# Shared last groups, a query projection one group ahead, V slots 0, 2, 5 or 0 on VectorE, 2 KB weight rows, and V sums ahead of two output projections

## The reference

```python
q = (xt @ w_q).reshape(t, PEER_HEADS, 2, PEER_HALF)
s = jnp.einsum("thpd,hpnd->thpn", q, sub_keys)          # 8 heads, 2 x 128 keys
s1, i1 = lax.top_k(s[:, :, 0], 16); s2, i2 = lax.top_k(s[:, :, 1], 16)
cand = s1[..., :, None] + s2[..., None, :]              # 256 candidates, again the best 16
idx, g = ..., softmax(top_s)                            # 16 experts a head and token
u = jnp.take(u_tab, ic, axis=0)                         # 16384 x 1024 table
a = jnp.einsum("cd,chkd->chk", xc, u)
w = gc * jax.nn.gelu(a, approximate=False)
vv = jnp.take(v_tab, ic, axis=0)
out = jnp.einsum("chk,chkd->cd", w, vv)
```

## Time and profile before

| | |
|---|---|
| median of 3 runs | 1631.06 us (1630.27 to 1631.42) |
| the profiled execution | 1630.2 us, of which its span is 1628.2 us |
| busy in the span | PE 1330.9 us, DVE 1073.0, POOL 1013.0, ACT 468.4 |
| moved by DMA | 619.20 MB, mean 380 GB/s; gathers 536.94 MB, SP's transfers 81.36 MB |
| granted TensorE clock, mean | 0.907 of full speed |

### The profile page before, as it was taken

How to read it: one execution, slowest core, us unless ns; L and a number is a source line. 1 busy time by engine, 2 the same in 40 slices (tenths; PEclk the granted TensorE clock), 3 DMA queues, 4 the chain that set the end, 5 groups by cost and what they waited for, 6 DMA issues and landing times.

```text
span 1628.2 us, 17186 instructions
## 1 busy us (share of the span) xinstructions
PE 1330.9 (82%) x4558; PEld 768.0 (47%) x4558; DVE 1073.0 (66%) x2529; ACT 468.4 (29%) x1427; POOL 1013.0 (62%) x1099
## 2 busy tenths in 40 slices
PE   7999789888885899887877789989868877777775
PEld 7887544444552564354444366545434432222222
DVE  4248689988775445638778835674878985555555
ACT  0203343333332222433233222451333321111112
POOL 0006677777547656667666654675776777777764
PEclk9999898999998999899888899999999988888887
DMA  9519999999999999999999999999999999999997
GB/s 336 185 53 372 397 399 409 405 404 405 379 391 378 396 393 394 409 405 390 401 401 403 401 376 384 397 397 393 400 403 409 409 411 409 410 409 410 410 409 272
DMA packets 224232, 619.20 MB, mean 380 GB/s; under 512 B 18914, under 2 KB 90652, under 8 KB 224156
## 3 DMA queue, kind: packets, MB, share of 16 engines
q0 software_dynamic: 147456, 536.94, 83.7%
q1 hardware_dynamic: 76699, 81.36, 15.0%
HBM read 617.17 MB, written 1.05 MB: 380 GB/s over the span
## 4 chain that ended last, share of the span: by engine, by line
PE 36%; DMA 22%; POOL 13%; issue 12%; DVE 9%; ACT 5%; POOLq 0%; SPq 0%; DVEq 0%; ACTq 0%
DMA u_ring<-in_peer_u_dram,idx_now 20%; PE acc L795 18%; PE tile L765 13%; POOL u_ring L520 7%; POOL v_ring L520 7%; DVE u_ring L1010 4%; ACT diag L610 2%; DMA v_ring<-in_peer_v_dram,idx_now 2%; ACT gelus L604 2%; PE xf L765 1%; PE tile L897 1%; PE tile L924 1%; PE tile L892 1%; PE tile L928 0%; PE tile L787 0%
## 5 line engine op out<-in xcount | busy, mean ns | idle before, releaser
L795 PE MATMUL acc<-v_ring,diag 128*128 128x512 f32 x1780 | 852.9, 637 | 118.5 <-ACT diag L610 74.0
L1010 DVE CUSTOM_DVE_ANT_0 u_ring<-u_ring,xf 128x1024 f32<-128x1024 f32 x512 | 613.2, 1216 | 270.2 <-DMA u_ring<-in_peer_u_dram,idx_now 267.2
L520 POOL DMA_INDIRECT v_ring<-in_peer_v_dram,idx_now x512 | 495.4, 968 | 294.5 <-issue 121.9
L795 PEld LDWEIGHTS acc<-v_ring,diag 128*128 128x128 f32 x1780 | 359.9, 207 | 581.3 <-issue 565.9
L520 POOL DMA_INDIRECT u_ring<-in_peer_u_dram,idx_now x512 | 503.3, 983 | 173.4 <-issue 126.5
L596 ACT ACTIVATE gelus<-dots 128x8 f32<-128x8 f32 x64 | 13.4, 209 | 515.4 <-DVE dots L1010 515.4
L610 ACT ACTIVATE diag<-ident,gelus 128x128 f32<-128x128 f32 x448 | 137.8, 388 | 2.1
L765 PE MATMUL tile<-w_ring,fT 128*128 128x256 f32 x480 | 110.4, 384 | 6.4 <-DVE fT L1159 6.4
L765 PEld LDWEIGHTS tile<-w_ring,fT 128*128 128x128 f32 x480 | 92.0, 192 | 30.3 <-issue 12.0
L604 ACT ACTIVATE gelus<-gelus,gates 128x1 f32<-128x1 f32 x512 | 102.1, 281 | 4.9 <-ACT gelus L596 3.3
L714 ACT ACTIVATE gexp<-best,gstat 128x16 f32<-128x16 f32 x32 | 9.8, 307 | 306.9 <-DVE best L1300 306.9
(11 more groups left out here) (170 smaller groups left out, 1043.0 us busy)
## 6 DMA issues: line engine op xcount, KB each, us to landing
w_ring<-in_peer_wq_dram SPq DMA_DIRECT2D x23, 1024.0 KB, 16.5
w_ring<-in_w_out_dram SPq DMA_DIRECT2D x12, 1024.0 KB, 16.8
w_ring<-in_w_kv_dram SPq DMA_DIRECT2D x12, 1024.0 KB, 16.9
u_ring<-in_peer_u_dram,idx_now POOLq DMA_INDIRECT x512, 11.5
v_ring<-in_peer_v_dram,idx_now POOLq DMA_INDIRECT x512, 11.0
w_ring<-in_w_in_b_dram SPq DMA_DIRECT2D x8, 1024.0 KB, 16.5
u_ring<-in_w_in_a_dram SPq DMA_DIRECT2D x4, 1024.0 KB, 12.2
w_ring<-in_w_mem_kv_dram SPq DMA_DIRECT2D x4, 1024.0 KB, 15.4
```

The lines of the kernel that those rows point to most:

```text
L520: pool.indirect_dma_start(ring[:, s, :], None, rows_[:, :], bass.IndirectOffsetOnAxis(idx_now[:, column + s:column + s + 1], 0), element_o ...
L795: ins = pe.matmul(acc[:, 512 * n:512 * n + 512], diag[:, par * G + s, :], v_ring[:, s, 512 * n:512 * n + 512], start=(first and s == 0), s ...
L1010: dve.tensor_tensor_reduce(u_ring[:, s, :], u_ring[:, s, :], xf[:, :], 1.0, 0.0, ALU.mult, ALU.add, dots[:, par * G + s:par * G + s + 1])\
```

## The change

1. **Who adds V slots.** `FOLDED` becomes [0]. In the groups `BUSY` (0 to 3 of phase 0, 0 to 9 of phases 1 and 2) DVE adds slots 0, 2 and 5 and PE the other five. In the last two groups DVE adds 1, 3, 5, 7 and 1, 3, 5, 6, 7 behind all dots (`fold_late` in place of `add_last`), with `read_sum` ahead of slot 6 of group 63. The final rows are made and stored in two halves of the columns.
2. **Query ahead.** The query projection and ACT's copy of it become a step of their own ("query"), which stands at the end of the side list of the group before its route. Some routes of phase 0 move by a group.
3. **Gathers.** `idx_now`, its copies and the loops on POOL go; gathers read `idx_all`. Phase 1 waits for the heads that a group needs.
4. **2 KB rows.** Pieces of out, q, k, v and qf are 512 rows by 512 columns: 1 MB again, in rows of 2 KB. A tile of 256 columns needs two pieces, which serve two tiles; both are held until the second tile is done.
5. **V sums ahead.** For groups 0 and 1 of phase 0, PE does the side steps up to the first "out", then the V sums, then the rest.

```diff
-FOLDED = [7]
+FOLDED = [0]
+LOOPED = GROUPS * PHASES - 2
+BUSY = [*range(0, 4), *range(GROUPS, GROUPS + 10), *range(2 * GROUPS, 2 * GROUPS + 10)]
+BUSY_FOLDED = [0, 2, 5]
+LATE_FOLDED = {LOOPED: [1, 3, 5, 7], LOOPED + 1: [1, 3, 5, 6, 7]}
...
+    pe_start, start = queried(pe_start), queried(start)
+    side[0, 0][0:0] = [("query", 0, 1)]
+    for key in list(side):
+        for step in [s for s in side[key] if s[0] == "route" and s != ("route", 0, 1)]:
...
+                side[key].remove(step)
+                side[key][0:0] = [step]
+                side[group_before(*key)].append(("query", *step[1:]))
...
+def split_side(ph, g):
+
+    steps = SIDE[ph, g]
+    cut = len(steps)
+    if (ph, g) in ((0, 0), (0, 1)):
+        cut = next(n for n, step in enumerate(steps) if step[0] == "out")
+    return steps[:cut], steps[cut:]
...
+        if len(key) == 4:
+            return blocks[:, key[3] * (KD // 2):(key[3] + 1) * (KD // 2), col:col + 2 * PC]
...
-            return HEADS * (ph // 2) + (HEADS if ph == 1 else h + 1)
+            return HEADS * (ph // 2) + h + 1
...
+            def gather_v(q, s):
+                if q == 0:
+                    filled(pool, LAST_USE[HELD[(G + s) // 2]])
+                elif s in folded(q - 1):
+                    pool.wait_ge(v_folded, folds_before(q - 1) + folded(q - 1).index(s) + 1)
+                else:
+                    pool.wait_ge(v_added, sums_before(q - 1) + summed(q - 1).index(s) + 1)
+                gather(v_rows, v_ring, q, s, v_landed)
...
+                elif kind == "query":
+                    _, ph, h = step
+                    filled(act, ("q", ph, h))
+                    act.activation(q_rows[:, :], bank(("q", ph, h))[:, 0:PC], ACT.Copy).then_inc(q_copied, 1)
...
-                    for step in SIDE[ph, g]:
+                    ahead, behind = split_side(ph, g)
+                    for step in ahead:
                         side(step)
                     if g == 0 and ph:
                         pe.wait_ge(acc_read, ph)
                     group(GROUPS * ph + g, g % 2, first=(g == 0))
+                    for step in behind:
+                        side(step)
```

More of the change, by code:

```diff
@@ L57, with folded, summed, counted @@
 NW = 5
-NI = 4
 WARM_UP = 15
-FOLDED = [7]
+FOLDED = [0]
 SUMMED = [s for s in range(G) if s not in FOLDED]
 GP, GD = len(SUMMED), len(FOLDED)
-PE_LAST = G // 2
+LOOPED = GROUPS * PHASES - 2
+BUSY = [*range(0, 4), *range(GROUPS, GROUPS + 10), *range(2 * GROUPS, 2 * GROUPS + 10)]
+BUSY_FOLDED = [0, 2, 5]
+LATE_FOLDED = {LOOPED: [1, 3, 5, 7], LOOPED + 1: [1, 3, 5, 6, 7]}
+def folded(q):
+    if not isinstance(q, int):
+        return FOLDED
+    return BUSY_FOLDED if q in BUSY else LATE_FOLDED.get(q, FOLDED)
+def summed(q):
+    return [s for s in range(G) if s not in folded(q)]
+def counted(q, slots):
+    if isinstance(q, int):
+        return sum(len(slots(n)) for n in range(q))
+    each, base = len(slots(LOOPED - 1)), GROUPS * (PHASES - 1) + 1
+    more = counted(base, slots) - each * base
+    return each * q + more
+def folds_before(q):
+    return counted(q, folded)
+def sums_before(q):
+    return counted(q, summed)
 ROUTE_PARTS = 2
@@ L511, in _, with gather @@
                                pattern=[[-1, P]], channel_multiplier=1).then_inc(consts_made, 1)
[L513 to L519, removed]
+            def gather(rows_, ring, q, s, landed):
+                ph, g = divmod(q, GROUPS)
+                col = (ph % 2) * P + G * g + s
                 pool.indirect_dma_start(
@@ L532, in held_used, with gather_u @@
[L532 to L552, removed]
-                    when(idx_copied, q + 2)
+            def gather_u(q, s):
+                ph, g = divmod(q, GROUPS)
+                if s == 0:
+                    pool.wait_ge(idx_made[ph % 2], heads_ready(ph, g // 2))
+                if q:
+                    pool.wait_ge(dot_done, G * (q - 1) + s + 1)
+                else:
+                    filled(pool, LAST_USE[HELD[s // 2]])
+                gather(u_rows, u_ring, q, s, u_landed)
@@ L575, in _ @@
-            for ph in range(PHASES):
-                first = 0
-                if ph == 0:
-                    for j in range(NI):
-                        group(ph, 0, j)
-                    first = 1
-                with pool.Fori(first, GROUPS // NI - 1) as i:
-                    for j in range(NI):
-                        group(ph, i, j)
-                for j in range(NI):
-                    group(ph, GROUPS // NI - 1, j, last=(ph == PHASES - 1 and j == NI - 1))
+                    gather_v(q, s)
@@ L788, in transposes, with group @@
                 done(ins)
[L790 to L792 removed]
+            def group(q, par, first=False):
+                for n_, s in enumerate(summed(q)):
+                    pe.wait_ge(diag_made, sums_before(q) + n_ + 1)
                     pe.wait_ge(v_landed[s], 16 * q + 16)
@@ L1371, in _ @@
                     side(step)
-            with dve.Fori(1, GROUPS // 2) as i:
+            with dve.Fori(1, GROUPS // 2 - 1) as i:
                 for par in range(2):
                     group(i * 2 + (base + par), par, last)
-            add_last()
-            read_sum(last)
+            for q in (LOOPED, LOOPED + 1):
+                group(q, q % 2, last)
+            fold_late()
             finish(1)
```

208 lines of the change are left out of this document (114 added, 94 removed).

## The result

The changed kernel takes 1687.55 us, the median of four runs (1682.74 to 1691.33), beside 1630.68 us for the kernel before (1630.27 to 1631.42). The ratio is 1.0347, with a 95% interval from 1.0315 to 1.0378: slower by 3.5%. The direction was forecast and the size was not: 57 us lost where 9 were forecast, and outside the range. The profiled execution took 1691.33 us, 61.1 more than the one before.

The account below looks back on a forecast made before the run. The prediction took the DMA engines as the bound: 1630.2 us less gains of 26.6 plus losses of 36 gave 1639.6, forecast as 1640 (0.5% slower), with a range of 1620 to 1655.

Parts of the forecast that it names:

- The bound: From 140 to 1580 us the DMA engines bound the kernel, with only about 9 us idle in 1440.
- The holes at groups 0 and 1: Gathers stop before V(1, 0) and again before V(2, 0): the DMA queue idles 21.5 and 12.5 us more.
- Groups 2 to 4 give DVE two more adds each: Early phase 0: 7.7 us more DVE work where it is already busy; loss taken as 2 us, 0 to 6.
- Two fewer slots on PE in busy groups: With queries ahead, shortens PE; can give back 0 to 6.5 us of idle DMA, 2.5 taken.
- Rival 5: DVE becomes the bound in phase 0, groups 2 to 7, costing 8 to 10 us more: 1649 us; chance 0.12.
- these shorten PE, not DMA: Fewer PE slots in busy groups and queries ahead can only recover idle DMA; 2.5 us gain taken for both.
- (b): Group 1: DVE waits for route (0, 1)'s exponential, now behind ACT's copy of query (0, 2); part of the 21.5 us hole.
- (c): Query (0, 2) on PE follows group 0's V sums and two outs; its pieces issue after out (1, 1); same 21.5 us hole.
- Wide rows: 2 KB rows cost 2.60 us a MB by interpolation; 52.4 MB of weights gain 16 us, between 0 and 24.
- The small gains: First gather earlier 0.9 us, phase 1 not waiting for all heads 2.5, the kernel's end 4.7.
- The end: Last group: gathers issued 2.8 us earlier, `acc` read ahead of the last add 1.3, half-size store 0.5; 4.7 in all.

Follow-up runs that it names:

- e10: e9 with pieces of 1024 rows by 256 columns (1 KB rows) for every matrix, as before: 1628.73 us, 0.9982 of the kernel before.
- e9: Kernel after with query projections directly ahead of their routes, V sums behind all side steps, and DVE adding slot 7 alone until the last two groups: 1617.6 us.
- e14: e9 with the change's V slots on DVE (0, 2 and 5 in busy groups, 0 elsewhere): 1632.2 us, 1.0006 of the kernel before.
- e8: Kernel after with every query projection and its copy directly ahead of its route, the route's rest at its place in the list: 1667.74 us.
- e1: Kernel after with V sums of groups 0 and 1 of phase 0 behind all side steps again: 1666.77 us, 1.0218 of the kernel before.
- e6: Kernel after with V sums behind all side steps, route (0, 1)'s exponential ahead of the next query's copy, and slot 7 alone on DVE: 1633.85 us.
- e3: Kernel after with V sums behind all side steps and route (0, 1)'s exponential ahead of the next query's copy: 1653.48 us, 1.0148 of the kernel before.
- e13: e9 with the last two groups' slots split as before (DVE adds 7, then 4 to 7): 1622.34 us, 0.9946 of the kernel before.
- e4: Kernel after with DVE adding one slot, 7, in all groups but the last two: 1664.86 us, 1.0212 of the kernel before.
- e5: Kernel after with DVE adding one slot, 0, in all groups but the last two: 1665.57 us, 1.021 of the kernel before.

## Why the prediction was right in sign and wrong in size

The experiments form a ladder from the kernel before to the kernel after, in which each step is one edit or one bundle:

| from, to | edit | us |
|---|---|---|
| before, e10 | direct gathers, heads a group at a time, new end, some routes moved | -2.0 |
| e10, e9 | 2 KB rows | -11.1 |
| e9, e14 | DVE's slots | +14.6 |
| e14, e8 | V sums ahead of the outs, in group 1 of route (0, 2) too | +35.5 |
| e8, after | queries a group ahead, the rest of a route first in its group | +19.8 |

The prices depend on the order: V sums ahead cost 20.8 when taken out of the kernel after (e1), where route (0, 2) stands ahead of them; queries ahead 16.3 between e9 and e6 and 21.3 between e14 and e3, with query (0, 2) ahead of the V sums and the exponential put first in e6 and e3; DVE's slots 14.6, 19.6 or 22.7.

**The bound: right.** The span less the idle time from 140 us to some 50 us before its end is 1599 to 1601 us in all kernels with wide rows (1604 in e13, whose end is longer) and 1619 in the two with 1 KB rows. And PE got 58 us less to do while the kernel got slower.

**The holes at groups 0 and 1: right in their links, and too small.** The exponential ran at 180.3 (forecast 177.0), V(1, 0) was issued at 184.4 (180.8), V(2, 0) 41.5 us later (37.8). From 140 to 235 us, where both holes lie, the DMA was idle 41.7 us more than before, where 34.0 were forecast for both. The 3.6 us of delay in the first chain come from two things. V(0, 7) was issued at 148.52 and not at 147.47, so the sums ended at 158.2 in place of 156.4. And the query projection took 5.55 us in place of 3.62, at a lower granted clock after PE had stood idle. Stretches of the kernel after:

```profile
158.00:165.20 7.20, 7.20 (x33) 5.89 (x31) 0.00 (x0) 0.00 (x0) 0.00 (x0) 1.00 0.01 2
...
173.00:176.00 3.00, 2.96 (x7) 2.46 (x8) 0.00 (x0) 0.00 (x0) 0.00 (x0) 0.50 0.00 0
...
173.00:179.00 6.00, 5.55 (x16) 4.30 (x16) 0.00 (x0) 0.38 (x1) 0.00 (x0) 0.68 0.00 0
```

The clock was at full speed (1.00, 2.4 GHz) while PE did the outs and at the lower level (0.50, 1.2 GHz) in the first 3 us after 7.8 us of idle PE; 0.68 is the mean of the two levels over the whole projection.

**Failed step 1, "Groups 2 to 4 give DVE two more adds each ... I take 2 us" and "Two fewer slots on PE in busy groups ... I take 2.5".** The 2.5 stood for PE's relief by the slots and by the queries together, so DVE's slots were booked at a net gain of at most 0.5 us; they cost 14.6 to 22.7. The step had the row that said so: DVE busy 19.5 of 20 us. Rival 5 drew the right conclusion but only for groups 2 to 7 and at 8 to 10 us, and missed phases 1 and 2. I judged a transfer of work from PE to DVE by PE's relief. The question was what ends the gathers' waits once DVE is later. A dot has to be done before each U gather in POOL's one queue, and e4 shows at groups 0 and 1 that this alone holds the stream up. In e14 most of POOL's wait for V slots is for DVE's adds, in e9 it is for PE's sums. Whether the load or the gate does it there was priced apart in the changed kernel alone (e5).

**Failed step 2, queries ahead: "these shorten PE, not DMA", in the same 2.5 us of gain.** They cost 16.3 to 21.3 us. Part of it was in the forecast, as (b) and (c) of the chain: the pieces of query (0, 2) are issued only when out (1, 1) is done. What was left out is that this remains when nothing stands in front of it: e6 waits 9.37 us for them ahead of the V sums. Further, the rest of a route now leads the list of its group, and PE meets ACT's second copy of it earlier, while that copy stands behind ACT's weights and diagonals of the same group: PE waits 149.6 us in all for this copy, 15.1 before, and 2.6 for the first copy, 86.7 before. Not every such wait costs. The one of 18.85 us (198.3) is nearly free: the V sums behind it need diagonals that ACT makes only from 196.45 on, and PE catches up with the gathers afterwards. Behind the one of 22.19 us (245.9) stand 9 us of other side work, and the V sums begin at 255.99, though ACT began their diagonals at 244.05. Whether the early query or the place of the route's rest costs more was not tested: every run moves both. Of the 20.9 us idle between 220 and 380 us, e4 (slot 7) has 14.5 left and e8 (queries beside) 10.7, so DVE's slots and the queries each have a share.

**Wide rows: price right, gain mis-sized.** 16 was forecast and 11.1 measured. The price is 2.58 us for a MB, close to the 2.60 interpolated, but about 4.9 us turned into idle. My term took the bytes' price as if every us saved were a us of the span.

**The small gains: a quarter of them.** Heads, direct gathers and the end were put at 0.9 + 2.5 + 4.7 = 8.1, and came to 2.0 in e10. Sharing the end gives 4.7 (e13) where 2.8 were forecast. Idle from 380 to 500 us fell by 1.7 to 1.9 in e10 and after (2.5 forecast); in e9, whose POOL waits for PE there, it rose, from 4.6 to 5.6. The 0.9 us of the first gather did not appear in the kernel after, where it is issued at 117.69 against 117.66 before, since its index is made later; in e10 it comes 1.1 us earlier. That leaves about 5 us of loss against these three in e10, whose cause I haven't found; the moved routes are in that step too.

**The end in the timeline.** POOL, then the last adds, in the kernel after:

```profile
1664.83 1.84 POOL L607 DMA_INDIRECT v_ring<-in_peer_v_dram,idx_all  x1 [3.26 <-PE acc L857]
...
1674.84 0.94 POOL L607 DMA_INDIRECT v_ring<-in_peer_v_dram,idx_all  x1 [0.30 <-issue]
...
1681.06 2.70 DVE L1105 SCALAR_TENSOR_TENSOR xres<-v_ring,gelus,xres 128x1024 f32<-128x1024 f32 x2
```

The eight issues take 10.0 us in place of 11.5, 8.7 in e10 as forecast. But from the last issue to the end of the span it is 14.76 us, with 14.66 before. The adds of slots 6 and 7 run back to back behind the read of `acc`, so neither the 1.3 us of the earlier read nor the 0.5 of the smaller store appeared.

In sum, the forecast for the kernel without holes (e3) would have been 1630.2 - 26.6 + 2 = 1605.6, and it took 1653.5. Of the 48 us, 36 are DVE's slots and queries ahead (e3 to e9), 5 are wide rows, and 6 the small gains. The 9 us forecast as the loss was the small difference of two sums of 26.6 and 36, of which the second was near only in its largest term.

## What to carry to other kernels

When one in-order queue feeds a saturated resource (here POOL's gathers and the DMA engines), list for every entry which engine releases it, and price any work moved onto that engine at its full duration wherever it also waits for others; a busy share of 70% doesn't mean slack. Work put "a step ahead" needs its inputs a step ahead too, and each engine's copy of it stands in front of something. Undo edits one at a time from both ends of the ladder: the best kernel here (e9, 1617.6 us, 0.8% faster than before) keeps the wide rows, the direct gathers and the shared end, and drops the three edits that cost 70 us together. And price a faster transfer by what it leaves idle: here a third of the saving did not reach the time.

## What the runs showed of the hardware

- The hardware queue moves 1 KB rows at 2.90 us for a MB and 2 KB rows at 2.58, beside gathers of 4 KB rows at 2.44. A fixed cost a row describes all three: it was set from the first and the last and gives 2.60 for the middle one.
- After idle stretches of PE the same projection of 16 matmuls took 5.55 us (7.8 idle before it) and 6.75 us (9.4 idle, e6) in place of 3.62, at a granted clock of 0.50 in the first 3 us after the idle time in both kernels. A hole in the gathers costs twice where PE's next work lies on the chain.
